# One landing buffer fewer and one rounding buffer more in a two-block transformer kernel

## The reference

```python
for layer in range(DEPTH):                      # first block
    mod = silu(c) @ mod_w[layer] + mod_b[layer] # 12 weight tiles of 1024 x 512 per layer
    x = x + g1 * mixer(rms_norm(x) * (1 + sc1) + sh1)
    x = x + g2 * moe(rms_norm(x) * (1 + sc2) + sh2)
# moe, per expert e: y = (silu(xb @ w1[e]) * (xb @ w3[e])) @ w2[e]
#   w1, w3: 1024 x 512, w2: 512 x 1024, fp32
for l in range(DEPTH):                          # second block
    x = x + 0.5 * swiglu(...); x = x + mixer2(...); x = x + 0.5 * swiglu(...)
```

## Time and profile before

| | us |
|---|---|
| median of 3 runs | 2197.49 (2195.88 to 2197.76) |
| profiled execution, own time | 2200.99 |
| its span, first to last instruction | 2199.2 |
| TensorE busy in it | 1999.7 (91%) |
| VectorE, ScalarE busy | 1445.8 (66%), 1129.5 (51%) |
| DMA: 457 MB, mean | 208 GB/s |

### The profile page before, as it was taken

One profiled execution on the slowest core, in us unless ns is written; L12 is line 12 of the kernel. 1 busy time (PEld: TensorE's weight loads), 2 busy tenths in 40 slices (PEclk: granted clock), 3 DMA queues, 4 the chain that ended last, 5 costly groups with the idle time before them and its releaser, 6 DMA issues.

```text
span 2199.2 us, 28139 instructions
## 1 busy us (share of the span) xinstructions
PE 1999.7 (91%) x11557; PEld 1696.3 (77%) x11557; DVE 1445.8 (66%) x1853; ACT 1129.5 (51%) x1491; POOL 75.3 (3%) x88
## 2 busy tenths in 40 slices
PE   4975899999977779999998999989999999989998
PEld 2844677878775567878778998769999999768997
DVE  2685588787876467878785655656555655566555
ACT  2442467676754257667674444545444444544443
POOL 0000001000000001000000000000000000000000
PEclk9996899999998779999999999989999999989999
DMA  8572688888857448888884555425555555424552
GB/s 311 181 274 100 230 278 292 273 292 280 297 175 246 144 159 289 286 281 287 285 305 137 192 182 194 138 76 173 186 183 185 177 190 192 154 77 148 188 181 101
DMA packets 209296, 457.33 MB, mean 208 GB/s; under 512 B 8816, under 2 KB 20744, under 8 KB 209160
## 3 DMA queue, kind: packets, MB, share of 16 engines
q1 hardware_dynamic: 204768, 450.99, 60.7%
q10 hardware_dynamic: 4392, 4.44, 0.6%
HBM read 454.35 MB, written 1.05 MB: 207 GB/s over the span
## 4 chain that ended last, share of the span: by engine, by line
PE 80%; DVE 12%; ACT 5%; issue 1%; DMA 1%; POOL 0%; SPq 0%; ACTq 0%; DVEq 0%; POOLq 0%
PE bank L257 78%; DVE rest L562 6%; ACT round L555 2%; PE bank L1756 2%; DVE arena L1099 2%; DVE catTl L1091 1%; DVE arena L1091 1%; DMA raw<-in_mod_w 1%; ACT arena L671 0%; DVE catTl L1099 0%; DVE arena L1496 0%; POOL G L618 0%; DVE acc L1091 0%; ACT hTh L703 0%; DMA raw<-in_ex_w 0%
## 5 line engine op out<-in xcount | busy, mean ns | idle before, releaser
L562 DVE TENSOR_TENSOR rest<-raw,round 128x1024 fp32r<-128x1024 f32 x758 | 889.6, 1221 | 383.5 <-ACT round L555 383.5
L555 ACT ACTIVATE round<-raw 128x1024 fp32r<-128x1024 f32 x758 | 758.6, 1053 | 516.6 <-PE bank L257 488.5
L257 PE MATMUL bank<-hTh,round 128*128 128x256 f32 x1600 | 450.0, 281 | 17.6 <-DVE hTl L1091 12.8
L257 PE MATMUL bank<-hTh,rest 128*128 128x256 f32 x1600 | 448.5, 280 | 0.0
L257 PE MATMUL bank<-hTl,round 128*128 128x256 f32 x1600 | 447.9, 280 | 0.0
L257 PEld LDWEIGHTS bank<-hTh,round 128*128 128x128 f32 x1600 | 301.6, 188 | 20.5 <-issue 19.7
L257 PEld LDWEIGHTS bank<-hTl,round 128*128 128x128 f32 x1600 | 301.7, 189 | 0.9
L257 PEld LDWEIGHTS bank<-hTh,rest 128*128 128x128 f32 x1600 | 302.2, 189 | 0.0
L257 PE MATMUL bank<-round,hTh 128*128 128x512 f32 x464 | 189.0, 407 | 8.1 <-DVE ms L1394 3.6
L257 PE MATMUL bank<-round,catTh 128*128 128x512 f32 x384 | 162.7, 424 | 36.9 <-DVE catTl L1091 25.7
L257 PE MATMUL bank<-rest,hTh 128*128 128x512 f32 x464 | 185.2, 399 | 0.0
(11 more groups left out here) (219 smaller groups left out, 2595.4 us busy)
## 6 DMA issues: line engine op xcount, KB each, us to landing
raw<-in_ex_w SPq DMA_DIRECT2D x192, 1024.0 KB, 5.5
raw<-in_mod_w SPq DMA_DIRECT2D x48, 1024.0 KB, 7.0
raw<-in_ffn_w_gate SPq DMA_DIRECT2D x44, 1024.0 KB, 5.2
raw<-in_ffn_w_up SPq DMA_DIRECT2D x44, 1024.0 KB, 5.1
raw<-in_ffn_w_down SPq DMA_DIRECT2D x44, 1024.0 KB, 4.8
raw<-in_w_in SPq DMA_DIRECT2D x20, 1024.0 KB, 5.1
raw<-in_ev_in_w SPq DMA_DIRECT2D x10, 1024.0 KB, 8.0
raw<-in_od_in_w SPq DMA_DIRECT2D x8, 1024.0 KB, 5.6
```

What stands on the lines that cost most here:

```text
L257: return e.matmul(o, l, r, start=start, stop=stop, skip_group_check=True)
L555: e.activation(hi[:, h], raw[:, h], ACT.Copy).then_inc(S("hi"), 1)
L562: e.tensor_tensor(lo[:, h], raw[:, h], hi[:, h].bitcast(F32), ALU.subtract).then_inc(S("lo"), 1)
```

## The change: constants of the two buffer pools

The pools keep their total size: nine buffers of 8 KB per partition. The look-ahead table, the slot of each piece, and the waits for `used` follow from the two numbers.

```diff
-NSLOT = 6
-NHI = 3
+NSLOT = 5
+NHI = 4
```

## The result

The changed kernel takes 2276.66 us in the median of four runs (2267.81 to 2279.54), the kernel before 2196.68 us (2192.78 to 2197.76) beside it: a ratio of 1.0361, 95% interval 1.0329 to 1.0392. It is slower by 80 us, where the forecast had 47 and the range ended at 2275. The profiled execution is the longest of the four, with 2279.54 us of its own and a span of 2277.7, 78.5 above that of the earlier trace rows.

What follows compares the result with a forecast made beforehand. TensorE, busy 91% of the span, was taken as the bound. Periods 31 us plus single places (2.3, 1.4, 2.3, 7.0, 2.0, 1.4) summed to 47.4, added to 2197.49: 2245 us, range 2212 to 2275.

Steps and rivals of the forecast that it cites:

- the large term: Expert periods: splits wait for transfers to land, 1.1 us in each of 28 periods, 31 us.
- the SwiGLU layers at nothing: SwiGLU layers: no cost, since pieces take 5.65 us each, a little over the 5.4 us transfer.
- the releasers named DMA: Expert periods, changed profile: ScalarE's split waits would name DMA as the releaser, where they named TensorE.
- The term of the periods: Expert periods: late landings at three places (`hidden`, `down`, `gathered`) cost 1.1 us a period, 31 us over 28.
- place 1: Expert period, ahead of `hidden`: the split waits for a fresh landing, +0.4 to +0.7 us at c'.
- The third rival: Expert periods: delays feed on each other and add up, 2.0 us a period, time 2270; chance 0.10.
- Start: Ahead of the first norm: four pieces stand instead of three while TensorE waits, +2.3 us.
- Convolution: Ahead of VectorE's 48 taps: the last `ev_out_w` piece lands later, at 173.2, so its split starts later, +1.4 us.
- First experts: Layer 0: five pieces instead of four ahead of `gate_hot`, +2.3; layer 1: -3.3 saved, +4.7 for five instead of three, net +1.4.
- Last experts: Each expert layer: `down` of the last but one expert stands behind a later-landing piece, +3.5 us, 7.0 in two layers.
- Odd mixer: Odd mixer: four pieces instead of three ahead of the copy; ScalarE's extra is not given back, +2.0 us.
- The second rival: Expert periods: the fourth buffer removes the 0.63 us wait ahead of c, 17.6 us in all, time 2180; chance 0.06.

Runs made afterwards that it cites:

- s4: Changed kernel with four landing slots instead of five, four rounding buffers, and the look-ahead table computed as for three buffers: 2267.39 us, ratio 1.0325.
- s6h4: Kernel before, room freed by moving constants and short stores, with a fourth rounding buffer and its longer look-ahead table, six landing slots kept: 2211.92 us, ratio 1.007.
- look2: Changed kernel (five landing slots, four rounding buffers) with the look-ahead table computed as for three buffers: 2174.97 us, ratio 0.9908.
- halves: Changed kernel with each expert piece's transfer issued as two of 512 KB, ScalarE rounding the first half once it lands: 2231.94 us, ratio 1.0163.
- hid5: Changed kernel with the split of the hidden values put ahead of the w1 weight pieces on ScalarE and VectorE: 2260.26 us, ratio 1.0283.
- lessB: Changed kernel with the look-ahead one piece shorter ahead of the gated output (`down`) alone, expert layers only: 2264.14 us, one run.
- look1: Changed kernel (five landing slots, four rounding buffers) with a look-ahead table of two pieces: 2285.69 us, ratio 1.0408.
- s5h3: Kernel before with five landing slots instead of six, three rounding buffers kept: 2202.29 us, ratio 1.004.
- s6h4l3: Kernel before, room freed by moving constants and short stores, with a fourth rounding buffer, six landing slots and the look-ahead table of three kept: 2171.4 us, ratio 0.9888.
- hid6: Kernel before with the split of the hidden values put ahead of the w1 weight pieces on ScalarE and VectorE: 2179.65 us, ratio 0.9919.
- lessC: Changed kernel with the look-ahead one piece shorter ahead of the gathered tokens alone, expert layers only: 2251.41 us, one run.
- lessM: Changed kernel with the look-ahead one piece shorter at all three places of an expert's period, expert layers only: 2180.53 us, ratio 0.992.
- s6h3r: Kernel before with two constants moved into a free gate row and two short stores moved to the arena, freeing room: 2198.83 us, ratio 1.0016.

## Why the prediction was wrong

The waits of the large term are right, its size is not. A split whose piece was issued at the use of i - 2 waits for the landing, and s4, s6h4, look2 and halves each show it. The sign, the SwiGLU layers at nothing and the releasers named DMA came as forecast; the starts in the chain, forecast 23.1 to 23.5 us apart, did not. Of the 31 us between the 78.5 of the two traces and the 47.4 of the sum, 20 are in the periods, 8 in the stretch to the convolution's end, 6 in the last experts and 1 in the first expert of layer 1, less 3 for the second block and 1 for the rest.

- **The term of the periods, 1.1 us.** Measured 1.7 above the kernel before, 45.3 us over the 26 periods between two c's, 51.1 with the two first c's, in place of 31 for 28. The step that failed is "Since SyncE issues at the same moments as before, only for another piece, the landings of before can be taken over as they stand": one delay was laid on a fixed timetable, place by place. But an issue hangs on a use, and a use now on a landing, so that the period is set by the lap. The rule "The delay of place 1 counts towards this" has the same fault; hid5 and lessB show that the wait taken from one place comes back at another. The third rival, delays that feed on each other, has nearly the right price (2.0) and the nearest time (2270); its reason, that they add up, is not what the runs show, so its number is near by luck.
- **Start, +2.3.** The wait grew from 10.81 to 13.09, the same in s6h4, and fell by as much in look1. Right.
- **Convolution, +1.4.** Right, in a stretch that came out 7.6 us too long for other reasons. The chain after the change:

```profile
169.69 12.70 DMA raw<-in_ev_out_w
...
185.86 0.60 DVE mrow L580
186.46 19.01 DVE arena L1099 x48
```

  The piece is issued at 169.69 (160.48 before), lands 12.7 us later as forecast, and ScalarE splits it at 182.41 (171.83 before): 1.4 us more than the delay that was there at its issue. The copy that the split has moved past (mrow) adds 0.6. The other 7 us are there before the issue, 5.4 of them by the clock, below. TensorE waits for the convolution less than before (13.73 for 15.33), because it comes later itself: it waits 5.22 us for a rest at the even mixer's output, where before has 3.18. The kernels with five slots (s5h3, look2, the changed one) all wait 5.22 to 5.24 there, s6h4l3 3.33, and another 0.5 to 0.6 for a piece of `mod_w`. In the changed kernel neither wait is on the chain; in s5h3, whose wait for the convolution stays 15.3, the one for the rest is.
- **First experts.** +1.8 for 2.3 in layer 0; in layer 1 the saved 3.3 (measured 2.5) and the 4.7 (4.9) look right. But the waits grew by 0.7 us in layer 0 (1.74 to 2.48) and by 2.8 in layer 1; the rest is matmuls of 0.63 us in place of 0.39, so the agreement is in part luck. The first c of each layer waits 3.08 and 2.90 us in place of 0.63, and the delay grows by 2.1 and 3.7 us there; the forecast gave it no more than any other period.
- **Last experts, +3.5 each.** Measured +5.6 in layer 0 and +7.4 in layer 1. The wait for catTl L1099 grew from 1.69 to 4.09, by 2.4 us, less than forecast. For what follows such a wait I had reckoned nothing, and it is as much again. TensorE's window behind that wait, up to the next one, after the change and then before:

```profile
650.55:662.77 12.22, 10.09 (x32) 0.78 0.28 93
```

```profile
609.24:619.07 9.83, 7.71 (x32) 1.00 0.63 224
```

  The next wait is 2.12 us in both, the same matmuls stand between, and they take 2.4 us more: from 651 to 655 us the granted clock is 0.50 of full speed (1.2 GHz) and a matmul takes 0.63 us, where before it is 1.00 (2.4 GHz) and 0.39. TensorE had been busy for 5.9 of the 10 us ahead of 650.55, before for 8.3 of the 10 ahead of 609.24. Layer 1 has the same, a little smaller: 3.92 for 1.70 us of wait, then 11.39 us for 9.84. Odd mixer: +2.0 as forecast (delay of 46.2 at 796.36, 44.2 at 672.11).
- **The second rival, the fourth buffer removes the wait ahead of c.** For this change I was right to set it aside, but for half a reason. I wrote that what fills the gap is "an order, not an allocation". It is both: look2 leaves the order as it was, adds the buffer, and the gap is gone, and hid6 removes it by order. The rule cited there (the Trainium skill, "Perfetto Trace Analysis", Optimization Strategy: the same gap again and again may mean too few buffers) agrees with look2's 259.00 of 259 us; s6h4 shows its limit, since a table that spends the buffer at once keeps the gap. The gain is more than 0.63, 0.83 a period; that the rest is what a matmul right behind a wait costs (0.50 us where its neighbours take 0.39) is argued only.

What stays open: why the landings on the chain take up to 6.74 us from 301 to 575 us when the median of all is 5.5, which of its laps takes six uses and which four, and how the 9.0 us ahead of the convolution divide in a typical execution.

## What to carry to other kernels

A look-ahead of as many pieces as there are buffers has no slack: every rounding then waits for the use just before. Give the planner one buffer less than the memory has, and the spare one removes the wait: the same two numbers with the table of three turn 80 us of loss into 22 us of gain. One less, not two: with the table of two (look1) the loss is back. And where a load is issued by a use, don't lay a delay on the old timetable: look for the loop (use, issue, landing, preparation, use), count the pieces it spans, and compare its lap with the time of these pieces. Here a lap of four uses, 15.4 to 17.8 us, stands against 4 x 21.4 / 6 = 14.3, what four pieces take when TensorE has no gap.

## What the runs showed of the hardware

The granted clock can fall at another place in executions that do the same up to there, and a longer wait can be followed by matmuls at half the clock: in the last experts of layer 0, above, they cost 2.4 us behind a wait that grew by 2.4. That the wait is what brings the clock down is not shown by a run of its own.

The changed kernel and lessC are one program up to the experts. Windows of TensorE (length, busy, granted clock, DMA share, GB/s), the changed kernel and then lessC:

```profile
114.00:124.00 10.00, 8.72 (x41) 0.79 0.35 111
124.00:134.00 10.00, 9.24 (x46) 0.69 0.37 117
```

```profile
114.00:124.00 10.00, 9.54 (x66) 1.00 0.48 156
124.00:134.00 10.00, 5.66 (x40) 1.00 1.05 392
```

In the first, 27 of the attention's matmuls (64x256) took 7.42 us from 119.69 on; in the second all 32 took 5.16 from 114.46 on. That is 5.4 us between the matmuls at 106.91 and 132.87 of the kernel before. lessM, hid5, lessB and lessC reach the first expert (251.16 before) 2.6, 1.8, 5.4 and -0.4 us after the kernel before, the profiled changed kernel 11.0 after it; s6h3r and hid6, which are the kernel before up to there, come 3.8 and 4.5 us ahead of it. So of the 11 us in the single pair of traces some 7 (4.1 as the mean of five, -2.8 as the mean of three) are the change's, an estimate, since the five spread from -0.4 to 11.0. A difference of a few microseconds at one place of one pair of traces is to be held against other executions of the same instructions before it is explained.
